# A PEER decoder trunk on one core: the h rows of each tile copied to PSUM, and two PSUM banks of each kind for the front instead of three

## The reference

```python
for l in range(DEPTH):
    h = rms_norm(x, attn_norm_w[l])
    proj = h @ w_in[l]                      # 1024 -> 3088 columns, split for the two head groups
    ...                                     # differential attention, chunked gated linear attention
    mix = concat(diff_o, gla_o)
    x = x + mix @ w_out[l]
    h = rms_norm(x, ffn_norm_w[l])
    x = x + peer(h, peer_w_q[l], peer_sub_keys[l], peer_u[l], peer_v[l])

def block(xb):                              # in peer: 128 tokens
    q = (xb @ w_q).reshape(tb, 8, 2, 128)
    s = einsum('thcd,hckd->thck', q, sub_keys)
    top_s, top_i = top_k(s, 16)             # twice 16 keys, then the best 16 of their 256 sums
    ...
    u = u_tab[expert]                       # 128 tokens x 8 heads x 16 experts, 1024 wide
    act = gelu(einsum('td,thkd->thk', xb, u))
    w = gate * act
    return einsum('thk,thkd->td', w, v_tab[expert])
```

## Time and profile before

| | us |
|---|---|
| median of 3 runs | 3348.75 |
| lowest, highest | 3347.01, 3353.49 |
| profiled execution, span from first to last instruction | 3366.8 |
| POOL busy, whole run | 2267.3 |
| VectorE busy, whole run | 2274.4 |
| TensorE busy, whole run | 2658.0 |

### The profile page before, as it was taken

One profiled execution on the slowest core, in us unless ns is written; L12 is line 12 of the kernel. 1 busy time (PEld: TensorE's weight loads), 2 busy tenths in 40 slices (PEclk: granted clock), 3 DMA queues, 4 the chain that ended last, 5 costly groups with the idle time before them and its releaser, 6 DMA issues.

```text
span 3366.8 us, 25897 instructions
## 1 busy us (share of the span) xinstructions
PE 2658.0 (79%) x7200; PEld 1257.8 (37%) x7200; DVE 2274.4 (68%) x4952; ACT 737.2 (22%) x1644; POOL 2267.3 (67%) x2074
## 2 busy tenths in 40 slices
PE   7866778998888778987887868998888776666667
PEld 3444333444354333433344423334435332222222
DVE  1559964579579984668659994568758995455443
ACT  2411121223221121223221121223322111111111
POOL 0025677777766777777776677777776676777776
PEclk9888899999998899999999889999999898988989
DMA  5248999999999999999999899999999999999998
GB/s 185 75 172 301 345 345 408 406 405 368 361 388 351 379 341 400 407 407 362 350 396 381 325 361 384 405 406 393 358 389 368 335 328 350 346 370 371 368 362 332
DMA packets 351442, 1185.41 MB, mean 352 GB/s; under 512 B 37666, under 2 KB 38212, under 8 KB 351044
## 3 DMA queue, kind: packets, MB, share of 16 engines
q0 software_dynamic: 294912, 1073.87, 84.2%
q1 hardware_dynamic: 56388, 109.88, 8.9%
HBM read 1181.52 MB, written 2.10 MB: 352 GB/s over the span
## 4 chain that ended last, share of the span: by engine, by line
POOL 27%; PE 23%; DVE 20%; issue 17%; DMA 11%; another core or an unknown queue 1%; ACT 1%; DVEq 0%; POOLq 0%; ACTq 0%
POOL v_ring L468 13%; POOL u_ring L468 13%; PE peer_acc L1258 12%; DMA v_ring<-in_peer_v,experts 8%; PE act_bank L1045 5%; DVE u_ring L986 4%; DMA u_ring<-in_peer_u,experts 4%; PE dve_bank L1045 2%; DVE work L752 2%; DVE work L741 1%; DVE work L749 1%; DVE work L738 1%; DVE work L931 1%; DVE work L933 1%
## 5 line engine op out<-in xcount | busy, mean ns | idle before, releaser
L1258 PE MATMUL peer_acc<-v_ring,diag 128*128 128x512 f32 x3584 | 1805.4, 645 | 647.1 <-DMA v_ring<-in_peer_v,experts 296.7
L986 DVE SCALAR_TENSOR_TENSOR u_ring<-u_ring,h 128x1024 f32<-128x1024 f32 x1024 | 1255.2, 1226 | 841.2 <-DMA u_ring<-in_peer_u,experts 730.1
L468 POOL DMA_INDIRECT v_ring<-in_peer_v,experts x1024 | 1146.9, 1120 | 524.3 <-issue 259.6
L468 POOL DMA_INDIRECT u_ring<-in_peer_u,experts x1024 | 1114.9, 1089 | 561.2 <-issue 308.9
L1258 PEld LDWEIGHTS peer_acc<-v_ring,diag 128*128 128x128 f32 x3584 | 688.5, 203 | 1647.7 <-issue 1009.4
L669 ACT ACTIVATE diag<-ident,wts 128x128 f32<-128x128 f32 x896 | 325.8, 397 | 1180.5 <-PE peer_acc L1258 580.9
L1045 PE MATMUL act_bank<-w_ring,hT 128*128 128x512 f32 x768 | 346.4, 598 | 0.7 <-ACT hT L508 0.7
L1045 PEld LDWEIGHTS act_bank<-w_ring,hT 128*128 128x128 f32 x768 | 147.5, 193 | 187.0 <-issue 185.6
L996 DVE SCALAR_TENSOR_TENSOR xs<-v_ring,wts,xs 128x1024 f32<-128x1024 f32 x128 | 164.5, 1285 | 49.5 <-DMA v_ring<-in_peer_v,experts 40.0
L1132 PE MATMUL act_bank<-hT,w_ring 128*128 128x256 f32 x768 | 175.6, 384 | 0.0
L1132 PEld LDWEIGHTS act_bank<-hT,w_ring 128*128 128x128 f32 x768 | 148.6, 194 | 39.4 <-issue 20.9
(11 more groups left out here) (158 smaller groups left out, 1540.0 us busy)
## 6 DMA issues: line engine op xcount, KB each, us to landing
w_ring<-in_w_in SPq DMA_DIRECT2D x24, 2048.0 KB
w_ring<-in_peer_w_q SPq DMA_DIRECT2D x16, 2048.0 KB
w_ring<-in_w_out SPq DMA_DIRECT2D x8, 2048.0 KB
u_ring<-in_peer_u,experts POOLq DMA_INDIRECT x1024
v_ring<-in_peer_v,experts POOLq DMA_INDIRECT x1024
xs<-in_x SPq DMA_DIRECT2D x4, 512.0 KB, 7.2
keysT<-in_peer_sub_keys SPq DMA_DIRECT2D x2, 1024.0 KB
out<-xs SPq DMA_DIRECT2D x4, 512.0 KB
```

What stands on the lines that cost most here:

```text
L468: pool.indirect_dma_start(ring[:, n % depth, :], None, table, bass.IndirectOffsetOnAxis(ap=experts[:, tile % TILES, e:e + 1], axis=0),).th ...
L986: tell(nc.vector.scalar_tensor_tensor(out=row, in0=row, scalar=1.0, in1=h2[:, tile % TILES, :], op0=ALU.mult, op1=ALU.mult, accum_out=dots ...
L1258: ins = nc.tensor.matmul(peer_acc[:, j * 512:(j + 1) * 512], diag[:, (v_count(c, s) - 1) % DIAGS, :], v_ring[:, n % V_RING, j * 512:(j + 1 ...
```

## The change

Three edits. First, a PSUM tensor `h_now` of two banks is added; before the first u product of each tile VectorE copies the tile's 1024 h values per partition there, and the u products of that tile read `h_now` in PSUM in place of `h2` in SBUF. Second, the front gets two banks of each kind instead of three, so that the total stays at eight; a fill then waits for the emptying two fills back. Third, some parts move: the second tile's turning of q and k (`QK_FLIP_AT`) by one part, attention (`ATTN_AT`) by one, the linear attention (`GLA_AT`) by two and by one, and one routing step one part earlier; a front has 137 parts instead of 136.

```diff
-ACT_BANKS = 3
-DVE_BANKS = 3
+ACT_BANKS = 2
+DVE_BANKS = 2
...
-    ATTN_AT = QK_FLIP_AT + HALF + 1
+    ATTN_AT = QK_FLIP_AT + 2 * HALF
...
-    GLA_AT = (LR_AT + 2, LR_AT + 16)
+    GLA_AT = (LR_AT + 4, LR_AT + 17)
...
-    groups += [(QK_FLIP_AT + i, 2, "qkT") for i in tiles for _ in range(2)]
+    groups += [(QK_FLIP_AT + 2 * i, 2, "qkT") for i in tiles for _ in range(2)]
...
-    groups += [(QUERY_AT, 0, "route"), (QUERY_AT + 2, 1, "route")]
+    groups += [(QUERY_AT, 0, "route"), (QUERY_AT + 1, 1, "route")]
...
         peer_acc = ctx.enter_context(nc.psum_tensor("peer_acc", [P, D], F32))
+        h_now = ctx.enter_context(nc.psum_tensor("h_now", [P, D], F32))
...
             def slot_u(c, s):
                 tile, n = c // PH, c * SLOTS + s
+                if n % (PH * SLOTS) == 0:
+                    link(nc.vector.tensor_copy(h_now[:], h2[:, tile % TILES, :]))
                 dve.wait_ge(u_landed[n % U_RING], 16 * (n // U_RING + 1))
                 row = u_ring[:, n % U_RING, :]
                 tell(nc.vector.scalar_tensor_tensor(
-                    out=row, in0=row, scalar=1.0, in1=h2[:, tile % TILES, :],
+                    out=row, in0=row, scalar=1.0, in1=h_now[:],
                     op0=ALU.mult, op1=ALU.mult, accum_out=dots[:, c % 2, s:s + 1]), u_used, "u_used")
```

More of the change, by code:

```diff
@@ L552, in front @@
                         yield
-                    if p == QUERY_AT + 3:
+                    if p == QUERY_AT + 2:
                         empty(scores[:, 0, 0])
@@ L556, in front @@
                         empty(lrT[0:RANK, :], HTOK, RANK)
-                    i = p - QK_FLIP_AT - 1
-                    if 0 <= i < HALF:
+                    i, off = divmod(p - QK_FLIP_AT - 1, 2)
+                    if off == 0 and 0 <= i < HALF:
                         empty(qT[:, :, i * P:(i + 1) * P])
@@ L1093, in front @@
                         ins.then_inc(act_filled, 1)
-                    i = p - QK_FLIP_AT
-                    if 0 <= i < HALF:
+                    i, off = divmod(p - QK_FLIP_AT, 2)
+                    if off == 0 and 0 <= i < HALF:
                         pe.wait_ge(qk_ready, k * HALF + i + 1)
@@ L1105, in front @@
                             flip_tile(mix[:, i, :])
-                        if p == QUERY_AT + 2 and i == 0:
+                        if p == QUERY_AT + 1 and i == 0:
                             pe.wait_ge(keys_loaded, 16 * (l + 1))
```

## The result

The median is 3440.8 us (four runs, 3436.3 to 3452.0) for 3351.1 us before, on the same chip: a ratio of 1.026, 95% interval [1.023, 1.029]. The forecast was 3282 us with a range of 3210 to 3345, so it was wrong, and in the direction too. The span of the profiled execution went from 3366.8 to 3434.5 us.

A forecast was written before the change was run, and what follows sets the result against it. The prediction took POOL to bound the tail, VectorE the routing, and 405 GB/s of DMA as ceiling. It summed -97 (gathers) + 5 (copies) + 25 (banks) = -67 us, to 3282 us, range 3210 to 3345.

The forecast's parts named there:

- The gathers stop standing: On POOL, 336.7 us of gathers' time is standing behind VectorE; 270 us of it, behind u products, was to go.
- The gain of 97 us that reaches the end: Over the whole kernel, the part of 270 us less standing that shortens the run: 41 + 42 + 14 = 97 us.
- The tail: From 2800 us to the end POOL was taken as the bound, the DMA as next: 41 us gained.
- The three "POOL-bound" stretches: At 800 to 900, 1500 to 1700 and 2300 to 2500 us, gathers below the 405 GB/s ceiling: 42 us gained.
- the rest (14): Stretches at the DMA ceiling, bound by VectorE, or mixed: 8% of the remaining 171 us, 14 us gained.
- Copies, +5: Eight copies of h to PSUM on VectorE, 10 us, half where VectorE has no slack: 5 us lost.
- PSUM operand, 0: The u product on VectorE takes as long with h in PSUM as in SBUF: 0 us.
- Banks, +25: In the fronts, 64 more fills wait for a bank at 0.78 us each, half counted: 25 us lost.
- Moved parts, "hidden by the slots around them": In the fronts, parts moved up to two places later cost nothing, since a front's end stays within one part.
- The lockstep rival: From q and k turning through attention, TensorE waits on emptying engines, 2.0 us a tight fill, 128 us: 3385 us; chance 7%.
- the DMA rival: The DMA engines already bound the kernel, so only 24 of the 97 us come: 3355 us; chance 7%.
- The prediction's reading ("meets such a product about 0.13 us after its start"): On POOL, a gather meeting a two-SBUF-input VectorE product about 0.13 us after its start stands until that product ends.

The follow-up runs named there:

- e3: Kernel before with each u product replaced by a sum over the landed row, without h (three banks, old places): ratio 1.001.
- e10: Kernel before with gathers of half a row each and u products replaced by a sum over the ring slot, without h: ratio 0.996.
- e6: Kernel after with its copies to PSUM kept, but u products reading h in SBUF: ratio 1.017 to the kernel before.
- e2: Kernel after with u products reading h in SBUF and no copies (two banks of each kind, moved parts): ratio 1.018 to the kernel before.
- e13: Kernel after with a rest on POOL, a memset of 256 values a partition, behind each v gather: ratio 1.015 to the kernel before.
- e11: Kernel before with the moved parts, three banks of each kind, and u products replaced by a sum over the landed row, without h: ratio 1.008.
- e1: Kernel before with the moved parts alone (three banks of each kind, h read in SBUF): ratio 1.006.
- e17: e3 with a rest on POOL, a memset of 256 values a partition, behind each v gather: ratio 0.998 to the kernel before.
- e14: Kernel after with one long rest on POOL in every eight slots, four memsets of 384 values: ratio 1.030 to the kernel before.
- e18: Kernel before with a short rest on POOL, a memset of 32 values a partition, behind each v gather: ratio 1.005.
- e9: Kernel before with gathers of half a row each, products still over the whole ring slot: ratio 1.009.

## Why the prediction was wrong

- **The gathers stop standing** (336.7 us, some 270 of it by u products): right. Busy time over 0.94 us a gather fell from 337 to 83 us, by 254 (before by the earlier trace rows).
- **The gain of 97 us that reaches the end**: this is the step that failed. Taken by itself, on three banks and the old places, it is 1.001, +5 us (-3 to +12). The tail was to give 41 us since "POOL is the bound; what is late next is the DMA". The first half was right: half rows show POOL as the bound where gathers stand. The second was not: next is the wait for `v_used`, often late and in bursts, and of the 42 us that POOL saved there 32 turned into idle time. Over the whole run of e3 POOL's waits for it grew from 244 to 465 us while its busy time fell by 282. The three "POOL-bound" stretches (42 us) and the rest (14) were sized by GB/s against 405, a ceiling that e10 shows not to be the one in force: with half the bytes the gathers come no faster, neither in the stretch of 405 GB/s nor in the tail.
- **Copies, +5**: not to be told from nothing (e6 against e2, within some 19 us). **PSUM operand, 0**: right, 1221 for 1226 ns.
- **Banks, +25**: 40 us (26 to 54), so too small. It comes in few long waits, not as 64 times 0.78 us; whether it lies on the act side is not shown.
- **Moved parts, "hidden by the slots around them"**: failed, 20 us (13 to 28).
- **Not in the sum at all**: fast gathers beside two banks, 0.008, 27 us (12 to 42; after against e2). The traces have 25 us more of VectorE's gaps in routing in after than in e2, and the rests of e13 give the time back (1.015, for 1.018 of e2). But e3 and e11 have 27 and 40 us of gaps and lost next to nothing by them, so why fast gathers cost time beside two banks stays open.

With the sizes measured: 20 + 40 + 27 = 87 us, and 0.026 x 3351 = 87. The three are steps of one chain, before, e1, e2, after, so they must add up; the sum proves no mechanism. The lockstep rival was partly right: banks and parts, 60 us, are what it would have had at 0.9 us a tight fill, and I gave it 7%. Its own condition, 1.4 us or more a fill, was not met: with the 97 us real, the kernel would still have been faster. But no rival had the other half, that the gain is nil and has a cost of its own.

Of the DMA rival: it said next to no gain too, and for a wrong reason. A share of 0.96 and GB/s near the top did not mean a bound; only half the bytes told.

What is shown and what is not: that a short rest in each slot removes bursts and gaps, and wins time although POOL gets busier, is shown twice (e13, e17). Fewer bursts alone don't win time: e14 has half as many as after and isn't faster, e18 has about half as many as before and is slower. So how much of the missing 97 us the late increments hold stays open. In the traces every burst arrives with POOL between gathers (before 26 of 26, after 51 of 51), a median of 1.8 and 2.5 us after the last one ended. That back-to-back gathers hold the increments up is one reading, and it isn't shown: in a burst POOL often waits for the same increment, and of the increments that are not late 290 of 515 in after arrive while a gather runs. It isn't shown either which path they share, nor whether the rest or the semaphore step that goes with it does the work. The Trainium skill (Perfetto Trace Analysis, the per-engine timelines) says that TensorE's end in a profile is an estimate and that its semaphore update is pushed after PSUM has acknowledged the writes and then has to propagate. Where in that the up to 8 us lie no run here shows. That the lateness is no matter of the recording alone is seen from ScalarE and POOL, which stand until the increments come.

## What to carry to other kernels

A stall that is taken away is worth what the next wait leaves of it: before forecasting, look for what paces POOL once it is fast, and price that, here the increments that POOL itself waits for. A high DMA share is no proof of a DMA bound; halving the bytes of a transfer is a cheap test, if nothing else that the transfer waits for moves with it. Buffers are worth more than averages suggest: one slot less in each ring cost 60 us, one bank less of each kind 40, in the banks' case by few, long waits.

## What the runs showed of the hardware

- A semaphore increment of TensorE arrives 0.015 us after the recorded end of a matrix product (median). But 121 of the 680 recorded before and 169 of the 684 after came over 0.5 us behind the last product that had ended, up to 7.2 and 7.7 us; in bursts of two to four. (896 were made; the rest are not in the traces.) ScalarE's `diag_ready` and VectorE's `u_used` hardly show it (over 0.5 us: 1 of 535 and 1 of 581 before, 1 of 548 and 5 of 544 after), VectorE's wait for its own step does in the gaps (7 before, 20 after). The two need not go together: e9 has 19 us of gaps with 12 bursts.
- Late increments are more frequent where gathers don't stand (e3: 207 of 681, e10: 286 of 696) and rarer with a rest in each slot (e13: 84 of 663, e17: 56 of 646, e18: 61 of 685).
- A VectorE operation with one tensor in PSUM never held a gather: 535 gathers of after start inside a u product that has over 0.3 us to go, and none takes over 0.96 us. Before there are 429 such gathers, and each takes 1.1 us or more. A `tensor_reduce` of one SBUF row doesn't hold them either (e3: 502 such gathers, none over 0.96 us).
- What holds a gather is a product that began before it. Before, 50 gathers have a u product running 0.13 us after their start that began no more than 0.04 us ahead of them, and none of the 50 stands. The prediction's reading ("meets such a product about 0.13 us after its start") is too wide by these.
- Half a row for each index, 2 KB for 4, changed neither a gather's time on POOL (0.95 us on average in e10's tail, 0.96 in e3's) nor, without the standing, the pace of the tail: 2.84 us a slot in both.
